# Gated mixers: half-width signed level steps on VectorE without GpSimd, row transposes between the levels, the output norm split by token half

## The chip, the cores and the metric

The kernel runs on one core of one Trainium2 chip, as one launch. The metric is the device time of one execution in microseconds, from its first to its last work on the core; a comparison takes the median of several runs. TensorE multiplies matrices into PSUM (eight banks of 128 x 512 fp32 values), VectorE (DVE), ScalarE (ACT) and GpSimd (POOL) work on rows of 128 partitions, SyncE (SP) starts the DMAs that bring the weights. The engines run programs of their own and meet only at semaphores.

## What is computed

A model of four layers on 256 tokens of width 1024, in fp32: a short convolution with gated DeltaNet, a mixture of 32 experts, a mixer of retention and gated linear attention (GLA), a dense SwiGLU block, an HGRN2 mixer, a mixture of 8 experts, a norm. The change touches the GLA and retention mixer and the HGRN2 mixer, which share this core:

```python
def gated_chunkwise(q, k, v, log_f):          # chunks of 64 tokens
    g_cum = jnp.cumsum(_to_chunks(log_f), axis=-2)
    def step(state, inp):
        qc, kc, vc, gc = inp
        diff = gc[:, :, :, None, :] - gc[:, :, None, :, :]
        decay = jnp.exp(jnp.where(mask, diff, -jnp.inf))
        scores = jnp.einsum('bhid,bhjd,bhijd->bhij', qc, kc, decay)
        g_last = gc[:, :, -1:, :]
        o = (jnp.einsum('bhij,bhjv->bhiv', scores, vc)
             + jnp.einsum('bhid,bhdv->bhiv', qc * jnp.exp(gc), state))
        state = (jnp.exp(g_last[:, :, 0, :])[..., None] * state
                 + jnp.einsum('bhjd,bhjv->bhdv', kc * jnp.exp(g_last - gc), vc))
        return state, o
# hgrn2: o = rms_norm(o, norm_g) * silu(g);  then @ w_out, added to the residual
```

GLA has 4 heads with keys of 64 values and values of 128. HGRN2 has 8 heads of 128, which the kernel takes as two halves of 4 heads. Retention has the same recurrence with a constant decay per head.

## The kernel before

**Layout.** A head's channels lie on the 128 partitions, its 256 tokens along the row; four heads are 1024 columns. Two GLA heads share one 256-column block of keys (`padded`), so that keys, decays and queries are 512 columns; the queries are spread over 1024 with the other head's channels zeroed by a mask.

**Levels.** The pairwise decays inside a chunk of 64 are made in `NL` = 6 levels of block sizes 32, 16, 8, 4, 2, 1, after a round 0 for the diagonal. At level n every block of 2 x size tokens has an older and a newer half. `gated_difference` (L2072) subtracts from the summed log decays g their value at the last token of the older half (the edge), over the full width; `gated_scalar_round` (L2055) makes exp(-|difference|) of it in two activations; `scaled_queries` (L2085, products L2090 and L2095) multiplies the queries by it on VectorE and `gated_pool_round` (L2065, L2069) the keys on GpSimd; `scores` (L2031, L2036) makes 16 matmul instructions of eight 128 x 128 products; `take_scores` (L2113) copies under a mask, with a predicated copy (L2121) over all 1024 columns, the pairs (older key, newer query) of this level into `c_AT`. Round 0 takes the diagonal (L2118). Scores of round n lie in banks 4 and 5 for even n, in 6 and 7 for odd n.

**Behind the levels.** `gated_vector_end` (L2125) makes g minus its last value of the chunk (L2133), the queries times exp(g), and the decays of whole chunks; `gated_scalar_end` (L2143) their exponentials (L2147 to L2151) and, after the transposes, the eviction of the key rows into two masked copies `c_kd` (L2157); `gated_pool_end` (L2161, L2163) the keys for the state; `gated_tensor_end` (L2166) transposes these to rows (`k_rows`, L2173, L2177) and calls `attend_tensor` (L2182).

**Attend.** Four chunks c: the state products Sp (L2198), VectorE's state S (L2239, L2241), the outputs o (L2215 from the state, L2217 from the scores) in banks 6 and 7. Between them `out.fill(1)` puts one quarter of the next projection (L508 to L510) or one block of the output projection (L638). Then the norm over all 1024 columns: square (L2260), sum by a matmul with ones (L2225), Ln and Exp (L2263, L2265), gain and gate on VectorE (L2250, L2253), which is y.

**What runs beside it.** The projections are made of three fp32r matmuls each; for that ScalarE rounds each quarter of a weight piece (`weights_hi_of`, L547) and GpSimd subtracts it from the original (`weights_lo_of`, L557), 128x1024 a piece. In GLA and in the first hgrn half TensorE has half a projection (`proj`) between the scores of two rounds, and in GpSimd's program the products of a round and two weight quarters alternate. On VectorE rounds 4 to 6 of the first hgrn half also have the forget gate of the second (L2846, L2847, reciprocal L2851). In the second half only output blocks lie between the rounds. `cumulate` (L2524) sums the log decays. The order on every engine is the order of its program; SP's loads wait for the last use of their slot.

Of the kernel before, what the change touches and what calls it, by code (L numbers as in the profile page):

```python
# [8 lines left out]
I32 = mybir.dt.int32  # L9
# [130 lines left out]
def program(nc, known, A):  # L140
# [3 lines left out]
    with ctx:  # L144
# [1870 lines left out]
        c_lb, c_omlb = c_small[:, 24:32], c_small[:, 32:40]  # L2015
        NL = len(LEVELS)

        class Gated:
            def __init__(self, st, tag, nb, q, k, g, v, gate, y, gain):
                self.st, self.tag, self.nb = st, tag, nb  # L2020
                self.q, self.k, self.g, self.v, self.gate, self.y, self.gain = q, k, g, v, gate, y, gain
                self.N = nb * T
                self.w = [w[:, 0:self.N] for w in c_w]
                self.kt = c_kt[:, 0:self.N]
                self.padded = nb == 2

        def parity(ap, par):

            return ap.rearrange("p (b r t) -> p b r t", r=2, t=T)[:, :, par, :]

        def scores(pe, x, name, k, q, b0):  # L2031

            for h in range(H4):
                for t in range(NT):
                    kb = k[:, (h if x.nb == 4 else h // 2) * T + t * P:(h if x.nb == 4 else h // 2) * T + t * P + P]
                    mm = nc.tensor.matmul(inst(bank(b0, 2), h, t), kb, inst(q, h, t), start=True, stop=True)  # L2036
            mm.then_inc(*E[x.st].step())
            E[x.st].name(x.tag + name)

        def gated_tensor_round(pe, x, n):  # L2040

            v, tag = V[x.st], x.tag
            b0 = 4 + 2 * (n % 2)
            if n == 0:
                pe.wait_ge(*v.at(tag + "ready"))
                scores(pe, x, "r0", x.k, c_qt if x.padded else x.q, b0)
            else:
                pe.wait_ge(*v.at(f"{tag}q{n}"))
                pe.wait_ge(*G[x.st].at(f"{tag}k{n}"))
                if n >= 2:  # L2050

                    pe.wait_ge(*v.at(f"{tag}taken{n - 2}"))
                scores(pe, x, f"r{n}", x.kt, c_qt, b0)

        def gated_scalar_round(act, x, n):  # L2055
# [4 lines left out]
            nc.scalar.activation(w, w, ACT.Abs).then_inc(*s.step())  # L2060
            act.wait_ge(*s.last())
            nc.scalar.activation(w, w, ACT.Exp, scale=-1.0).then_inc(*s.step())
            s.name(f"{x.tag}w{n}")

        def gated_pool_round(pool, x, n):  # L2065
            pool.wait_ge(*S[x.st].at(f"{x.tag}w{n}"))
            if n >= 2:
                pool.wait_ge(*E[x.st].at(f"{x.tag}r{n - 1}"))
            nc.gpsimd.tensor_tensor(x.kt, x.k, x.w[n % 2], ALU.mult).then_inc(*G[x.st].step())  # L2069
            G[x.st].name(f"{x.tag}k{n}")  # L2070

        def gated_difference(dve, x, n):  # L2072
# [3 lines left out]
            g = x.g.rearrange("p (b i) -> p b i", i=2 * size)  # L2076
            if n >= 3:

                dve.wait_ge(*G[x.st].at(f"{x.tag}k{n - 2}"))
            nc.vector.tensor_tensor(x.w[n % 2].rearrange("p (b i) -> p b i", i=2 * size), g,  # L2080
                                    g[:, :, size - 1:size].to_broadcast([P, x.N // (2 * size), 2 * size]),
                                    ALU.subtract).then_inc(*v.step())
            v.name(f"{x.tag}d{n}")

        def scaled_queries(dve, x, w, scale=1.0):  # L2085

            v = V[x.st]
            if x.padded:
                for par in range(2):
                    ins = nc.vector.scalar_tensor_tensor(  # L2090
                        parity(c_qt, par), x.q.rearrange("p (b t) -> p b t", t=T),
                        consts[:, C_HALF + par:C_HALF + par + 1], w.rearrange("p (b t) -> p b t", t=T),
                        ALU.mult, ALU.mult).then_inc(*v.step())
            else:
                nc.vector.tensor_tensor(c_qt, x.q, w, ALU.mult).then_inc(*v.step())  # L2095

        def gated_vector_round(dve, x, n):
# [3 lines left out]
            if n < NL:  # L2101
                if n >= 1:
                    dve.wait_ge(*v.last())
                gated_difference(dve, x, n + 1)
            if n >= 1:
                dve.wait_ge(*s.at(f"{tag}w{n}"))
                if n >= 2 or x.padded:
                    dve.wait_ge(*e.at(f"{tag}r{n - 1}"))
                scaled_queries(dve, x, x.w[n % 2])
                v.name(f"{tag}q{n}")  # L2110
                take_scores(dve, x, n - 1)

        def take_scores(dve, x, n):  # L2113
            e, v = E[x.st], V[x.st]
            b0 = 4 + 2 * (n % 2)
# [3 lines left out]
            else:  # L2119
                mask = level_mask(n - 1).bitcast(I32).unsqueeze(1).to_broadcast([P, 8, P])  # L2120
                nc.vector.copy_predicated(blocks(c_AT), mask, blocks(bank(b0, 2))).then_inc(*v.step())  # L2121
            v.name(f"{x.tag}taken{n}")
            dve.wait_ge(*v.last())

        def gated_vector_end(dve, x):  # L2125

            e, s, v = E[x.st], S[x.st], V[x.st]
            tag = x.tag
            take_scores(dve, x, NL)

            dve.wait_ge(*G[x.st].at(f"{tag}k{NL}"))
            chunks = x.g.rearrange("p (b i) -> p b i", i=CH)
            nc.vector.tensor_tensor(x.w[0].rearrange("p (b i) -> p b i", i=CH), chunks,  # L2133
                                    chunks[:, :, CH - 1:CH].to_broadcast([P, x.N // CH, CH]),
                                    ALU.subtract).then_inc(*v.step())
            v.name(tag + "last")
# [891 lines left out]
```

## Time and profile before

| | |
|---|---|
| median of 3 runs | 2338.02 us (2336.57 to 2338.24) |
| the profiled execution | 2338.94 us, span of its trace 2337.1 us |
| busy in the span | PE 2045.9 us (88%), DVE 629.3, ACT 502.7, POOL 289.4 |
| chain that ended last | PE 69%, DMA 17%, DVE 8%, ACT 3%, issue 2%, POOL 1% |
| DMA | 653.03 MB, 279 GB/s over the span |

The page gives busy times over the whole span. PE is busy nearly everywhere, but its share differs by stage: the experts are fed at some 420 GB/s, the mixers load little and wait for each other's engines. A row of the chain tells which engine the end of the kernel hung on at that moment; a row of the timeline tells what an instruction waited for.

### The profile page before, as it was taken

Reading aid. Unit: us, or ns where it says so; the run is one execution under the profiler, and the core shown is the slowest. Engines: PE = TensorE matmul, PEld = TensorE weight load, DVE = VectorE, ACT = ScalarE, POOL = GpSimd, SP = SyncE. Lnnn points to the kernel's source line nnn. Section 1 sums busy time; section 2 is a strip of 40 time slices with the busy share of each in tenths; the row PEclk is TensorE's granted clock in tenths of the full one; section 3 lists DMA queues with packets and bytes.
Section 4 is the critical chain, followed back from the end, with each engine's and each line's share of the span. In section 5 each row is a group of like instructions: output and inputs, shape, how many; then the busy total and the mean of one; then the engine's idle time right before and its main releaser. Section 6 shows DMA issues by size and latency. Waiting matters only on the chain.

```text
span 2337.1 us, 38525 instructions
## 1 busy us (share of the span) xinstructions
PE 2045.9 (88%) x16903; PEld 1291.4 (55%) x16903; DVE 629.3 (27%) x983; ACT 502.7 (22%) x641; POOL 289.4 (12%) x118
## 2 busy tenths in 40 slices
PE   6889788787877897999897767999999899999998
PEld 6888544333434886899897655343344334333434
DVE  4662311111112661444377522000001000100101
ACT  3521121211113442343355321000000000000001
POOL 4630000000001560000177310000000000000000
PEclk8999688888888998999998777999999999999999
DMA  7322299999999330355542204899999999999991
GB/s 263 109 109 77 96 424 424 424 424 424 424 424 379 107 110 19 129 179 188 190 145 109 108 1 149 313 388 418 419 417 420 418 419 419 418 420 418 411 390 55
DMA packets 134330, 653.03 MB, mean 279 GB/s; under 512 B 9776, under 2 KB 32432, under 8 KB 88880
## 3 DMA queue, kind: packets, MB, share of 16 engines
q1 hardware_dynamic: 134192, 650.95, 70.0%
q8 instruction: 116, 1.90, 0.3%
q14 instruction: 22, 0.18, 0.0%
HBM read 649.86 MB, written 1.05 MB: 279 GB/s over the span
## 4 chain that ended last, share of the span: by engine, by line
PE 69%; DMA 17%; DVE 8%; ACT 3%; issue 2%; POOL 1%; SPq 0%; POOLq 0%; DVEq 0%; ACTq 0%
PE psum L1748 16%; DMA ring<-in_w_down 14%; PE psum L1810 8%; PE psum L1754 5%; PE psum L508 5%; PE psum L509 5%; PE psum L510 5%; PE psum L638 4%; PE psum L1554 3%; PE psum L1815 3%; DMA ring<-in_moe_w_down 2%; PE psum L2036 2%; PE psum L1775 2%; PE psum L1731 1%; DVE hT L491 1%
## 5 line engine op out<-in xcount | busy, mean ns | idle before, releaser
L1748 PE MATMUL psum<-ring,arena 128*32 128x384 f32 (+1 forms) x3584 | 369.1, 542 | 3.3 <-DMA ring<-in_moe_w_up 2.6
L557 POOL TENSOR_TENSOR ring_r<-ring,ring_r 128x1024 fp32r<-128x1024 f32 x88 | 224.7, 2570 | 969.0 <-ACT ring_r L547 968.9
L510 PE MATMUL psum<-ring_r 128*128 128x256 f32 x1056 | 301.1, 285 | 0.0
L1748 PEld LDWEIGHTS psum<-ring,arena 128*32 128x32 f32 x3584 | 114.3, 110 | 222.5 <-issue 213.0
L508 PE MATMUL psum<-ring_r 128*128 128x256 f32 x704 | 206.8, 294 | 17.5 <-POOL ring_r L557 9.6
L1810 PE MATMUL psum<-ring,arena 128*32 128x512 f32 x1600 | 201.0, 605 | 8.6 <-DMA ring<-in_moe_w_down 8.4
L510 PEld LDWEIGHTS psum<-ring_r 128*128 128x128 f32 x1056 | 205.0, 194 | 0.0
L509 PE MATMUL psum<-ring_r 128*128 128x256 f32 x704 | 201.8, 287 | 0.0
L1954 DVE TENSOR_TENSOR arena<-arena,psum 128x512 f32<-128x512 f32 (+1 forms) x42 | 23.7, 616 | 508.4 <-PE psum L1754 359.4
L1511 PE MATMUL psum<-ring,arena 128*32 128x512 f32 x1024 | 141.9, 707 | 19.6 <-DMA ring<-in_w_up 19.6
L508 PEld LDWEIGHTS psum<-ring_r 128*128 128x128 f32 x704 | 138.4, 197 | 21.0 <-issue 11.4
L1533 PE MATMUL psum<-arena 64*128 64x256 f32 x272 | 99.1, 537 | 45.5 <-ACT arena L1593 45.5
L509 PEld LDWEIGHTS psum<-ring_r 128*128 128x128 f32 x704 | 138.3, 196 | 1.0 <-issue 1.0
L1754 PE MATMUL psum<-ring,arena 128*32 128x512 f32 (+1 forms) x1120 | 131.5, 542 | 0.0
L1893 ACT ACTIVATE arena<-psum 128x512 f32<-128x512 f32 (+1 forms) x42 | 20.0, 544 | 467.0 <-PE psum L1785 467.0
L547 ACT ACTIVATE ring_r<-ring 128x1024 fp32r<-128x1024 f32 x88 | 91.0, 1055 | 119.6 <-PE psum L510 119.6
L1533 PEld LDWEIGHTS psum<-arena 64*128 64x128 f32 x272 | 69.6, 264 | 66.9 <-issue 47.5
L508 PE MATMUL psum<-ring_r,arena_r 128*128 128x256 f32 x352 | 99.9, 284 | 5.5 <-DVE ring_r L533 5.5
L1511 PEld LDWEIGHTS psum<-ring,arena 128*32 128x32 f32 x1024 | 36.3, 127 | 121.0 <-issue 121.0
L638 PE MATMUL psum<-arena,ring 128*128 128x256 f32 x384 | 93.7, 402 | 9.9 <-DVE arena L2253 9.9
L1659 DVE TENSOR_TENSOR xT<-xT,psum 128x512 f32<-128x512 f32 x68 | 46.7, 687 | 206.4 <-PE psum L1533 206.4
L509 PE MATMUL psum<-ring_r,arena_r 128*128 128x256 f32 x352 | 99.8, 283 | 0.0
(370 smaller groups left out, 2779.8 us busy)
## 6 DMA issues: line engine op xcount, KB each, us to landing
ring<-in_w_gate SPq DMA_DIRECT2D x64, 1024.0 KB, 15.8
ring<-in_w_down SPq DMA_DIRECT2D x32, 2048.0 KB, 21.0
ring<-in_w_up SPq DMA_DIRECT2D x64, 1024.0 KB, 19.9
ring<-in_moe_w_gate SPq DMA_DIRECT2D x64, 1024.0 KB, 22.4
ring<-in_moe_w_down SPq DMA_DIRECT2D x64, 1024.0 KB, 21.0
ring<-in_moe_w_up SPq DMA_DIRECT2D x48, 1024.0 KB, 18.8
ring<-in_moe_w_gate SPq DMA_DIRECT2D x64, 768.0 KB, 20.6
ring<-in_moe_w_up SPq DMA_DIRECT2D x48, 768.0 KB, 21.3
```

Of the source, the lines that this page charges most:

```text
L508: nc.tensor.matmul(out, ah, bh, start=start, stop=False, **kw)
L509: nc.tensor.matmul(out, ah, bl, start=False, stop=False, **kw)
L510: return nc.tensor.matmul(out, al, bh, start=False, stop=stop, **kw)
L547: nc.scalar.activation(w_hi[:, :, c], w[:, :, c], ACT.Copy).then_inc(*S[st].step())
L557: nc.gpsimd.tensor_tensor(lo[:, :, c], w[:, :, c], w_hi[:, :, c].bitcast(F32), ALU.subtract)\
L638: mm = nc.tensor.matmul(bank(b // 2)[:, (b % 2) * T:(b % 2 + 1) * T], w[:, k, (b % 4) * P:(b % 4 + 1) * P], self.src[:, k, :], start=(firs ...
L1511: mm = nc.tensor.matmul(bank(0)[s * C:(s + 1) * C, :], q_Xg[:, k * PC + x * C:k * PC + (x + 1) * C], w[s][:, k, :], start=(k == 0), stop=( ...
L1533: mm = nc.tensor.matmul(bank(5 - r % 2)[:, j * T:(j + 1) * T], q_y[:, k * P:(k + 1) * P], q_shareT, start=True, stop=True)
L1554: mm = nc.tensor.matmul(bank(2)[at:at + C, :], q_hidT[:, f * PC + x * C:f * PC + (x + 1) * C], w[x][:, f, half * 512:(half + 1) * 512], st ...
L1748: mm = nc.tensor.matmul(bank(b0 + j)[n * MORE:(n + 1) * MORE, 0:Q], z_Xg[:, x:x + MORE], w[:, (2 * h + j) * Q:(2 * h + j + 1) * Q], start= ...
L1754: mm = nc.tensor.matmul(bank(b0 + 2)[q * MORE:(q + 1) * MORE, 0:Q], z_Xg[:, x:x + MORE], w[:, q * Q:(q + 1) * Q], start=(k == 0), stop=(k ...
L1810: mm = nc.tensor.matmul(bank(6)[tile * MORE:(tile + 1) * MORE, :], z_hidT[:, x:x + MORE], rows_of(half, 0, 512), start=first, stop=last)
```

## The change

- The differences are taken with a sign that is never positive, older half edge - g and newer half g - edge, as two instructions of half width; ScalarE needs one Exp per round and no Abs.
- Queries are scaled in the newer halves and keys in the older halves only, both on VectorE; keys (and for the unpadded mixers queries too) are double-buffered. GpSimd keeps only the weight rounding.
- The predicated copies act on the newer columns alone.
- The difference to the chunk's last value is taken in round 0; its Exp and that of g come in ScalarE's round 1, the state keys in VectorE's round 1, the decayed queries in round 2; the key rows are transposed before the scores of round 3, in banks of their own turn, and evicted after ScalarE's round 3.
- The padded layout puts a head's two masked copies in contiguous halves of 512. Two buffers move into `hT`, which is free in these stages.
- Outputs of chunks 0, 1 and of 2, 3 go to banks 6 and 7; square, sum, Ln, Exp, gain and gate act per token half, and the first half's sum stands between chunks 2 and 3; chunk 2 is given two fills.
- In hgrn the factor of q goes into the keys' factor. The rotation of the retention mixer moves to banks 4 and 5.

```diff
+        BANK_USES = ["r0", "r1", "r2", "kr"] + [f"r{n}" for n in range(3, NL + 1)]
...
+        def wait_for_bank(pe, x, use):
+            at = BANK_USES.index(use)
+            if at >= 2:
+                before_ = BANK_USES[at - 2]
+                pe.wait_ge(*(S[x.st].at(x.tag + "kd") if before_ == "kr" else V[x.st].at(f"{x.tag}taken{before_[1:]}")))
...
         def gated_tensor_round(pe, x, n):
+            if n == 3:
+                pe.wait_ge(*v.at(tag + "kl"))
+                wait_for_bank(pe, x, "kr")
+                k_rows(pe, x, x.kl, bank_of("kr"))
...
         def gated_scalar_round(act, x, n):
-            nc.scalar.activation(w, w, ACT.Abs).then_inc(*s.step())
-            act.wait_ge(*s.last())
-            nc.scalar.activation(w, w, ACT.Exp, scale=-1.0).then_inc(*s.step())
+            nc.scalar.activation(w, w, ACT.Exp).then_inc(*s.step())
             s.name(f"{x.tag}w{n}")
+            if n == 1:
+                act.wait_ge(*v.at(x.tag + "last"))
+                nc.scalar.activation(x.kl, x.kl, ACT.Exp).then_inc(*s.step())
+                s.name(x.tag + "el")
+                nc.scalar.activation(x.eg, x.g, ACT.Exp).then_inc(*s.step())
+                s.name(x.tag + "eg")
...
         def gated_difference(dve, x, n):
+            nc.vector.tensor_tensor(older(w, size), edge, older(x.g, size), ALU.subtract).then_inc(*v.step())
+            nc.vector.tensor_tensor(newer(w, size), newer(x.g, size), edge, ALU.subtract).then_inc(*v.step())
...
         def gated_vector_round(dve, x, n):
+                    dve.wait_ge(*v.at(f"{tag}z{n - 1}" if n >= 2 else f"{tag}last"))
+                gated_difference(dve, x, n + 1)
+            if n == 0:
+                chunks = x.g.rearrange("p (b i) -> p b i", i=CH)
+                nc.vector.tensor_tensor(x.kl.rearrange("p (b i) -> p b i", i=CH),
+                                        chunks[:, :, CH - 1:CH].to_broadcast([P, x.N // CH, CH]), chunks,
+                                        ALU.subtract).then_inc(*v.step())
+                v.name(tag + "last")
+                return
+            dve.wait_ge(*s.at(f"{tag}w{n}"))
+            if x.padded or n >= 2:
+                dve.wait_ge(*e.at(f"{tag}r{n - 1 if x.padded else n - 2}"))
+            if x.padded:
+                masked_queries(dve, x, w, q, lambda ap: newer(ap, size))
+            else:
+                nc.vector.tensor_tensor(newer(q, size), newer(x.q, size), newer(w, size), ALU.mult).then_inc(*v.step())
+            nc.vector.tensor_tensor(older(k, size), older(x.k, size), older(w, size), ALU.mult).then_inc(*v.step())
+            v.name(f"{tag}z{n}")
+            take_scores(dve, x, n - 1)
+            if n == 1:
+                dve.wait_ge(*s.at(tag + "el"))
+                nc.vector.tensor_tensor(x.kl, x.k, x.kl, ALU.mult).then_inc(*v.step())
+                v.name(tag + "kl")
+            elif n == 2:
+                dve.wait_ge(*s.at(tag + "eg"))
+                nc.vector.tensor_copy(c_decay[:, 0:4 * x.nb], x.eg[:, CH - 1::CH]).then_inc(*v.step())
...
+                    nc.vector.tensor_tensor(x.qd, x.q, x.eg, ALU.mult).then_inc(*v.step())
+                v.name(tag + "qd")
...
+                at, new = (newer(ap, size).rearrange("p (n b) i -> p n b i", n=8) for ap in (c_AT, bank(b0, 2)))
+                nc.vector.copy_predicated(at, mask, new).then_inc(*v.step())
...
-        def gated_pool_round(pool, x, n):
-        def gated_vector_end(dve, x):
-        def gated_scalar_end(act, x):
-        def gated_pool_end(pool, x):
-        def gated_tensor_end(pe, x, out=None):
...
         def attend_tensor(pe, x, out=None):
+            def sums(t):
+                pe.wait_ge(*s.at(f"{tag}osq{t}"))
+                mm = nc.tensor.matmul(bank_heads(5 - t), ones[:, :], by_time(c_AT, t), start=True, stop=True)
...
-                    out.fill(1)
+                    out.fill(2 if c == 2 else 1)
...
+                if c == 2:
+                    sums(0)
             if out:
                 out.fill(2)
+            sums(1)
...
         def attend_scalar(act, x):
+            for t in range(NT):
+                at = by_time(c_AT, t)
+                act.wait_ge(*e.at(f"{tag}o{2 * t + 1}"))
+                nc.scalar.activation(at, bank_heads(6 + t), ACT.Square).then_inc(*s.step())
...
-                do(nc.vector.tensor_scalar(x.q, x.q, float(P) ** -0.5, None, ALU.mult))
```

## Rows read from the trace of the kernel before

**Rows 1.** windows: us, busy PE, PEld, DVE, ACT, POOL; PE clock, DMA share, GB/s

```profile
795.00:933.00 138.00, 119.36 (x862) 111.16 (x863) 70.25 (x72) 51.42 (x67) 57.73 (x26) 0.96 0.26 85
1201.00:1395.00 194.00, 144.66 (x953) 132.88 (x953) 105.28 (x102) 74.40 (x79) 93.81 (x32) 0.83 0.22 83
1442.00:2300.00 858.00, 841.58 (x8664) 335.36 (x8665) 60.84 (x124) 60.23 (x124) 0.00 (x0) 0.99 0.97 392
```

**Rows 2.** PE timeline behind the GLA rounds: start, us, what, idle before, releaser

```profile
852.66 1.95 PE L2311 MATMUL psum<-arena,consts 128*128 128x512 f32 x4 [1.57 <-DVE arena L2492]
...
862.15 2.05 PE L2198 MATMUL psum<-arena 128*128 128x128 f32 x16 [1.35 <-ACT arena L2157]
...
865.58 0.35 PE L508 MATMUL psum<-ring_r 128*128 128x256 f32 x1 [1.38 <-ACT ring_r L547]
...
885.51 1.98 PE L2225 MATMUL psum<-arena,ones 128*128 128x512 f32 x4 [1.11 <-ACT arena L2260]
...
892.52 3.75 PE L2036 MATMUL psum<-arena 128*128 128x128 f32 x16 [5.03 <-DVE arena L2253]
...
932.14 15.77 PE L638 MATMUL psum<-arena,ring 128*128 128x256 f32 x64 [4.95 <-DVE arena L2253]
```

**Rows 3.** chain that ended last, first and sixth GLA scores: start, us

```profile
795.50 2.05 PE psum L2036 x16
...
834.02 2.05 PE psum L2036 x16
```

**Rows 4.** the same chain, hgrn first half

```profile
1200.29 0.70 DVE arena L2875
...
1204.07 0.21 PE psum L508
...
1283.46 3.78 PE psum L2198 x16
...
1305.99 1.03 ACT arena L2260
...
1315.16 1.24 DVE arena L2080
```

**Rows 5.** timeline of PE in hgrn, both halves

```profile
1235.70 2.02 PE L2036 MATMUL psum<-arena 128*128 128x128 f32 x16 [0.26 <-issue]
...
1247.96 3.78 PE L2036 MATMUL psum<-arena 128*128 128x128 f32 x16 [3.96 <-DVE arena L2095]
...
1279.83 1.97 PE L2177 MATMUL psum<-consts,arena 128*128 128x128 f32 x8 [8.04 <-POOL arena L2163]
...
1322.18 3.75 PE L2036 MATMUL psum<-arena 128*128 128x128 f32 x16 [5.86 <-POOL arena L2069]
...
1355.45 2.02 PE L2036 MATMUL psum<-arena 128*128 128x128 f32 x16 [1.74 <-issue]
```

**Rows 6.** the same chain, hgrn second half

```profile
1369.35 3.57 PE psum L2198 x16
1372.92 1.73 PE psum L638 x8
...
1385.23 1.03 ACT arena L2260
...
1394.87 16.55 PE psum L638 x64
```

**Rows 7.** DVE groups by form, 1312 to 1358, then 1204 to 1260

```profile
L2121 DVE COPY_PREDICATED arena<-consts,psum 128x1024 f32<-128x1024 int32 x6 | 7.8, 1304 | 3.2 <-PE psum L2036 3.2
L2080 DVE TENSOR_TENSOR arena<-arena 128x1024 f32<-128x1024 f32 x6 | 7.4, 1226 | 4.7 <-POOL arena L2069 4.6
...
L2080 DVE TENSOR_TENSOR arena<-arena 128x1024 f32<-128x1024 f32 x4 | 11.3, 2830 | 3.7 <-POOL arena L2069 3.6
```

**Rows 8.** timeline, 512 columns on ACT and on DVE

```profile
791.91 0.60 ACT L2275 ACTIVATE arena<-psum 128x512 f32<-128x512 f32 x1 [0.81 <-PE psum L510]
...
787.48 0.69 DVE L2473 SCALAR_TENSOR_TENSOR arena<-arena 128x512 f32<-128x512 f32 x1 [1.36 <-ACT arena L2384]
```

More of the change, by code:

```diff
@@ L2143, in gated_scalar_end @@
-        def gated_scalar_end(act, x):
-            s, v = S[x.st], V[x.st]
-            tag = x.tag
-            act.wait_ge(*v.at(tag + "last"))
-            nc.scalar.activation(x.w[1], x.g, ACT.Exp).then_inc(*s.step())
-            s.name(tag + "eg")
-            nc.scalar.activation(x.w[0], x.w[0], ACT.Abs).then_inc(*s.step())
-            act.wait_ge(*s.last())
-            nc.scalar.activation(x.w[0], x.w[0], ACT.Exp, scale=-1.0).then_inc(*s.step())
-            s.name(tag + "el")
-            for b in range(x.N // 512):
-                act.wait_ge(*E[x.st].at(f"{tag}kr{b}"))
-                for half in range(2):
-                    nc.scalar.activation(c_kd[half][:, b * 512:(b + 1) * 512], bank(4 + b), ACT.Copy,
-                                         scale=consts[:, C_HALF + half:C_HALF + half + 1]).then_inc(*s.step())
-            s.name(tag + "kd")
@@ L2220, in attend_tensor @@
                 e.name(f"{tag}o{c}")
+                if c == 2:
+                    sums(0)
             if out:
                 out.fill(2)
-            pe.wait_ge(*s.at(tag + "osq"))
-            for half in range(2):
-                mm = nc.tensor.matmul(bank(4 + half), ones[:, :], c_w[0][:, half * 512:(half + 1) * 512],
-                                      start=True, stop=True)
-            mm.then_inc(*e.step())
-            e.name(tag + "osum")
+            sums(1)
         def attend_vector(dve, x, decay, meanwhile=None):
@@ L2233, in attend_vector @@
                 dve.wait_ge(*e.at(f"{tag}Sp{c}"))
+                if c:
+                    dve.wait_ge(*v.last())
                 if c > 1:
@@ L2392, in mixer2_scalar @@
                     keep(name, halves(out), parts=(part,), **kw)
+                    if n == 3:
+                        gated_scalar_rows(act, GLA)
                     n += 1
@@ L2397, in mixer2_scalar @@
             act.preload_act_table_set(EXP_LN)
-            gated_scalar_end(act, GLA)
             keep("av", halves(a_v))
@@ L2417, in mixer2_pool @@
         def mixer2_pool(pool):
-            def lo(name, quarters=range(4)):
-                weights_lo_of(pool, "mix2", "two", name, quarters)
-            lo("bqk")
-            lo("bv")
-            lo("aq", (0, 1))
-            n = 1
-            for name, after in (("aq", "ak"), ("ak", "bg"), ("bg", "av")):
-                gated_pool_round(pool, GLA, n)
-                lo(name, (2, 3))
-                gated_pool_round(pool, GLA, n + 1)
-                lo(after, (0, 1))
-                n += 2
-            lo("av", (2, 3))
-            gated_pool_end(pool, GLA)
-            lo("ag")
+            for name in ("bqk", "bv", "aq", "ak", "bg", "av", "ag"):
+                weights_lo_of(pool, "mix2", "two", name)
         def mixer2_vector(dve):
@@ L2783, in hgrn_scalar @@
                 gated_scalar_round(act, HG[1], n)
+                if n == 3:
+                    gated_scalar_rows(act, HG[1])
                 if n == 2:
@@ L2787, in hgrn_scalar @@
                     act.preload_act_table_set(EXP_LN)
[L2788 removed]
             attend_scalar(act, HG[1])
         def hgrn_pool(pool):
[L2792 to L2810 removed]
+            for name in ("hf0", "hq0", "hi0", "hg0", "hf1", "hq1", "hi1", "hg1"):
+                weights_lo_of(pool, "hgrn", "two", name)
         def hgrn_vector(dve):
```

224 lines of the change are left out of this document (104 added, 120 removed).

## The prediction

> **What bounds the kernel now.** I read the busy time of three stretches first [rows 1]. In the GLA and retention stretch (795 to 933) TensorE is busy 119 of 138 us; in the two hgrn halves (1201 to 1395) only 145 of 194, at a mean clock of 0.83; in the second mixture of experts (1442 to 2300) 842 of 858 with the DMA engines at 0.97. So the order of waits in the mixers matters, TensorE is what a shorter mixer must free, and the last stage is full from end to end. Then I read TensorE's waits in the GLA stage [rows 2] and its pace there [rows 3]: from the first scores to the sixth, 38.5 us for five rounds, 7.7 us each, of which 2.05 are scores and 5.65 half a projection. That is TensorE at work all the time: the rounds of the GLA stage have nothing to give. Its waits come behind them. For hgrn I read the chain that ended last [rows 4 and 6] and the waits [rows 5]: the reader is to see a wait of 8.0 us for GpSimd's last product, one of 4.0 in round 5, and in the second half the rounds, which have only output blocks beside them.
>
> **GLA and retention.** The rounds stay at 7.7 us. Three waits behind them lose their cause [rows 2]: 1.57 us (the rotated queries are late, because VectorE first waits for ScalarE's exponentials, behind the silu of the gate; these now sit in rounds 1 and 2), 1.35 us (the key rows are evicted) and 1.38 us (ScalarE stood in that eviction and rounded the next weights late). Together 4.3. The transposes are moved and not removed, and what ScalarE now does in round 3 (two copies of 0.6 us) lies beside 5.65 us of projection.
> The norm by halves: square, Ln, Exp and the two VectorE products each act on 512 columns, at 0.60 us on ScalarE and 0.69 on VectorE [rows 8] instead of about 1.05 and 1.25. The half for the first tokens goes under the fourth chunk; its sum is work that is moved. TensorE's wait for the square falls from 1.11 to 0.7, that for y from 5.03 to 2.9 (0.65 + 0.63 + 0.69 + 0.69 and handoffs) [rows 2], which is 2.5. In retention the wait of 4.95 falls to 2.9 likewise, 2.05; one output block is moved ahead of it at no cost. **Sum: 8.9 us.**
>
> **Hgrn, first half.** The scaling of q goes: 0.70 [rows 4], on the chain, since r0 waits for it. From the end of r0 (1204.07 [rows 4]) to r4 (1235.70 [rows 5]) 31.6 us pass. TensorE's own work is four halves of 5.65, three scores of 2.05, the moved transposes (1.0; eight took 1.97 at the half clock [rows 5]) and about 0.9 for matmuls at the lower clock behind r0 (its first took 0.21 us [rows 4]), 30.6: a gain of 1.0. Round 4 is new trouble: ScalarE must make four copies of 0.6 before the exponential of round 4, so VectorE's products come some 8.5 to 10.8 us after the transposes begin and TensorE wants them after 8.8; I take 1.0 off. The wait of 3.96 in round 5 [rows 5] I leave: it comes from the three instructions of the next forget gate (5.9 us), and behind them now stand four half-width instructions where two stood.
> After the last projection TensorE stands from 1271.8 to 1283.46 [rows 5, 4]: for the products of the state keys, then the transposes, then the eviction. All of it is done by round 4 now: 11.6. The first state products then run warm, 2.05 us [rows 2] where they took 3.78 [rows 4]: 1.7. From the last output to the end of y were 9.2 us (1305.99 to 1315.16 [rows 4]); now 1.0 for the moved sum, 0.7, a sum of 1.6 half cold, 2.66 and handoffs, 6.2: 3.0. **Sum: 0.7 + 1.0 − 1.0 + 11.6 + 1.7 + 3.0 = 17.0.** What covers the state keys' rows now is the projections of rounds 3 and 4; if that cover were gone the 2.4 us of copies would come back. Queued behind them on ScalarE are the exponential of round 4 and the rounding of weights.
>
> **Hgrn, second half.** No projection covers it. From the end of y (1315.16) to the first state products (1369.35) are 54.2 us [rows 4, 6]. VectorE now does per round: two half-width differences, two half-width products, each 0.70 (a 128x512 product of two took 0.69 [rows 8], so halves cost more than half of 1.23), and a half-width predicated copy, 1.30 − 0.53 = 0.77 [rows 7]: 3.6 us, no less than the 3.76 of before, but GpSimd's 3.4 us and its two handoffs are gone from the chain. Laid out from the end of y: difference 1, the state difference, difference 2 and products 1 end at 5.4 (r1 began 7.0 after y before [rows 5]); the diagonal copy 1.22, state keys 1.23, difference 3, products 2 at 10.65; copy, decayed queries, difference 4, products 3 and copy at 16.4, when r3 may start. ScalarE's four copies hold its exponential of round 4 until 18.6, products 4 end at 20.0. From there TensorE sets the pace, scores 2.02 [rows 5] and an output block 1.73 [rows 6]: r5 at 23.9, r6 at 27.7, its block done at 31.5. I add 1.5 because the clock is at its lower level after the waits at the start: r1 took 3.75 behind a wait of 5.9 [rows 5]. So 33.0 against 54.2: 21.2. Key rows, the last predicated copy, the exponentials behind it: none stand between r6 and the state products, which were 11.9 us apart (1357.5 to 1369.35). The first state products: 3.57 → 2.05, 1.5. The tail from 1385.23 to 1394.87 [rows 6] was 9.6, now 6.2: 3.4. The output projection after it took 16.55 for 64, where warm blocks of 1.73 would give 13.8; I take nothing, as a wait of 2.9 may keep it cold. **Sum: 26.1.**
>
> **The sum.** 8.9 + 17.0 + 26.1 = 52.0. The profiled execution took 2338.9 us (span 2337.1 and 1.8 around it), the median of the runs is 2338.0; taken off the median it gives 2286. No layer of loading eats it: the loads of the last stage's first weights begin when the hgrn projections free their slots, and move ahead with them; the stage is at its rate from the start [rows 1].
>
> **A rule against the trace.** A 128x1024 product of two SBUF operands took VectorE 1.23 us with GpSimd idle and 2.83 in the mean while GpSimd rounded weights [rows 7]. The Trainium skill ("SBUF — State Buffer", "SBUF: two separate sides") says why: VectorE instructions with two SBUF inputs and GpSimd share a port pair, and the one that starts first holds it for its whole instruction. The trace agrees. It speaks against splitting: each half can be held up anew. It is the first rival.
>
> **Rivals.**
> *The port holds the halves up.* Per round of the GLA stage and of the first hgrn half GpSimd still makes two products of about 2.4 us. If both hold VectorE up in full, its round is 3.6 + 4.8 = 8.4 us against TensorE's 7.7: 0.7 in each of twelve rounds, 8 us: 2294. For it: the 2.83 [rows 7]. Against: a third GpSimd product per round is gone, and one round of slack lies between products and scores.
> *The clock stays low in the second half.* If TensorE's waits of one to two us keep rounds 2 to 6 and the state products cold, scores cost 3.75 and blocks 3.5: five rounds of 7.3 instead of 3.8 to 5, some 13 us: 2299. For it: before, one round fell back (mean clock 0.83 [rows 1]); against, from r4 on TensorE has no wait.
> *It all goes well.* The round 5 wait shrinks by 4, its scores stay warm, the output projection runs warm (2.7 twice), round 4 is not late: 52 + 13, 2273.
> *Short strided runs are slow (the other side).* At the last levels the half-width patterns are runs of one or two values with gaps, which no row of before shows on VectorE. If each half-width instruction took dt longer, the second half loses 30 dt, the first 30 dt, GLA 36 dt less about 12 us of slack; the gain of 52 is eaten at dt = 0.67 us, that is if halves of 0.70 took 1.37, more than the full width did. At 0.8 the kernel would be at 2351. Against it: the full-width differences re-read one value per run at every level, down to runs of two, and all took 1.23 [rows 7]. A cost of 0.1 to 0.2 each is only part of the range. The Trainium skill ("SBUF — State Buffer", "Door 1: The DMA port swizzle") says that a 16-byte SBUF line wants two hits and that a PSUM line has two fp32 values; every second value of a bank is one hit per line, so by it the copy of the last level would be slow, three instructions in all, under 2 us if each took its former 1.30. No run here shows it.
>
> **How the numbers follow.** My forecast 0.50, the port 0.17, the low clock 0.10, all well 0.17, slow strided runs 0.03, gains lost elsewhere (a late weight, a new wait that leaves the time within 0.2% of before) 0.03. The range reaches over the port and low clock cases above and to 2268 below, where the halves would also cost 0.62 rather than 0.70: 2268 to 2302. Within 0.2% (4.7 us, what a measurement of this kernel can tell from no change) only the last case; slower only the strided one, in most of its sizes. Faster 0.95, same 0.02, slower 0.03.
>
> **What would show it.** Right: GpSimd left with weight rounding alone; GLA rounds still 7.7 us apart and no wait over 1 us until its squares; the first state products of the first hgrn half within 1 us of the last projection, those of the second some 33 us after y; waits of 2.9 for y. Wrong: strided products well over 0.70 with GpSimd idle; rounds of the first hgrn half over 8.4 us; a new wait of r3 for the copy before it or of r4 for the evicted rows.

## The result, and the profile after

| | before | after | ratio [95%] |
|---|---|---|---|
| medians (4 runs each) | 2338.13 us | 2285.16 us (2283.60 to 2288.95) | 0.9775 [0.9760, 0.9789] |
| predicted | | 2286 us (2268 to 2302) | |
| profiled execution | 2338.94, span 2337.1 | 2288.95, span 2287.0 | |

The kernel is faster by 53 us, one microsecond from the forecast. The sum behind it was less right than that: two of its terms missed, one by 5 us, and others made up for it. The spans, cut at instructions that both kernels have (PE's first GLA scores, its retention scores, the output projection of the retention mixer, VectorE's first scan, the end of y of the first hgrn half, the last output projection and its end), each number the difference of two starts:

| us | before | after | gain | forecast | paced (below) |
|---|---|---|---|---|---|
| up to the GLA scores | 795.5 | 795.5 | 0.0 | 0 | 795.3 |
| GLA | 97.0 | 95.5 | 1.5 | 6.8 | 88.8 |
| retention | 39.6 | 36.4 | 3.2 | 2.1 | 37.2 |
| output projection, dense block, forget gate | 260.8 | 259.3 | 1.5 | 0 | 259.0 |
| hgrn, scans to the first y | 122.2 | 107.0 | 15.2 | 17.0 | 95.4 |
| hgrn, second half | 79.7 | 51.2 | 28.5 | 26.1 | 50.5 |
| its output projection | 16.6 | 15.8 | 0.8 | 0 | 15.6 |
| all behind it | 925.7 | 926.3 | −0.6 | 0 | 924.5 |

The windows of after that answer to [rows 1] (columns as there) show TensorE with the same instructions in shorter stretches, at a mean clock of 0.92 in hgrn where it was 0.83, and VectorE and GpSimd with less work. (Warm and cold below stand for TensorE's two clock levels: the sixteen matmuls of a round's scores took 1.8 to 2.05 us warm and up to 3.8 cold.)

```profile
795.00:928.00 133.00, 119.19 (x863) 112.34 (x864) 56.91 (x89) 48.05 (x66) 44.50 (x19) 0.95 0.26 88
1195.00:1345.00 150.00, 129.47 (x953) 123.80 (x953) 92.89 (x138) 60.57 (x71) 41.70 (x17) 0.92 0.28 106
```

**GLA.** PE's waits in its timeline after, where [rows 2] had 1.57, 1.35, 1.38, 1.11, 5.03 and 4.95:

```profile
807.21 3.78 PE L2066 MATMUL psum<-arena 128*128 128x128 f32 x16 [3.96 <-DVE arena L2165]
...
886.81 1.12 PE L2239 MATMUL psum<-arena,ones 128*128 128x512 f32 x2 [0.69 <-ACT arena L2305]
...
890.98 3.51 PE L2066 MATMUL psum<-arena 128*128 128x128 f32 x16 [3.04 <-DVE arena L2297]
...
927.42 15.77 PE L638 MATMUL psum<-arena,ring 128*128 128x256 f32 x64 [2.95 <-DVE arena L2297]
```

The first three waits are gone and the norm's shrank as forecast. New is the first row: round 1 waits 3.96 us for VectorE's keys, and its scores then take 3.78 us where those of [rows 3] took 2.05. That is 5.7 us, more than the 5.3 by which the stage misses its forecast. VectorE's and GpSimd's timelines say why; the last line is GpSimd's in the kernel before:

```profile
795.98 2.87 DVE L2150 TENSOR_TENSOR hT<-arena 128x512 f32<-128x512 f32 x1
798.89 2.52 DVE L2129 TENSOR_TENSOR arena<-arena 128x256 f32<-128x256 f32 x1
801.33 0.41 DVE L2130 TENSOR_TENSOR arena<-arena 128x256 f32<-128x256 f32 x1
...
804.60 2.56 DVE L2165 TENSOR_TENSOR arena<-arena 128x256 f32<-128x256 f32 x1
```
```profile
795.92 5.20 POOL L557 TENSOR_TENSOR ring_r<-ring,ring_r 128x1024 fp32r<-128x1024 f32 x2 [0.82 <-ACT ring_r L547]
801.61 2.39 POOL L557 TENSOR_TENSOR ring_r<-ring,ring_r 128x1024 fp32r<-128x1024 f32 x1 [0.49 <-ACT ring_r L547]
```
```profile
798.60 1.29 POOL L2069 TENSOR_TENSOR arena<-arena 128x512 f32<-128x512 f32 x1 [3.43 <-ACT arena L2062]
```

A subtraction of 256 columns takes 0.41 us in one row and 2.52 in another: beside a weight quarter of GpSimd it waits that quarter out. Before the change GpSimd's program had its level product between the quarters, and so waited for ScalarE's exponentials there, 3.43 us before the one of round 1. Now it has only weights and runs through four quarters while VectorE is in rounds 0 and 1.

**First hgrn half.** VectorE's scans and GpSimd beside them (timelines), first before, then after:

```profile
1192.93 7.33 DVE L2524 TENSOR_TENSOR_SCAN arena<-ones,arena 128x64 f32<-128x64 f32 x16 [1.13 <-ACT arena L2754]
```
```profile
1193.92 4.73 POOL L557 TENSOR_TENSOR ring_r<-ring,ring_r 128x1024 fp32r<-128x1024 f32 x2 [5.01 <-ACT ring_r L547]
```
```profile
1186.74 11.56 DVE L2555 TENSOR_TENSOR_SCAN arena<-ones,arena 128x64 f32<-128x64 f32 x16 [1.13 <-ACT arena L2787]
```
```profile
1187.73 9.32 POOL L557 TENSOR_TENSOR ring_r<-ring,ring_r 128x1024 fp32r<-128x1024 f32 x4 [5.01 <-ACT ring_r L547]
```

PE's waits (timeline) and the chain that ended last, both after:

```profile
1198.35 3.71 PE L2066 MATMUL psum<-arena 128*128 128x128 f32 x16 [7.69 <-DVE arena L2555]
...
1244.16 3.78 PE L2066 MATMUL psum<-arena 128*128 128x128 f32 x16 [5.32 <-DVE arena L2165]
```
```profile
1267.80 1.78 PE psum L2232 x16
...
1293.74 0.60 DVE arena L2129
```

The first state products start as the last projection ends, at 1267.80 and warm (1.78 us); before they came 11.7 us after it and took 3.78 [rows 4]. Against that the sixteen scans take 11.56 us, with four weight quarters beside them, where they took 7.33 with two. TensorE's wait before round 0 is 7.69 us now.

**Second hgrn half**, same chain:

```profile
1309.66 2.42 ACT arena L2118 x4
1312.09 0.95 ACT arena L2103
...
1313.67 0.70 DVE arena L2165
1314.41 2.05 PE psum L2066 x16
...
1325.22 1.78 PE psum L2232 x16
```

From y (1293.74) to the first state products are 31.5 us where [rows 4, 6] had 54.2. Round 4 is set by ScalarE: its exponential comes behind the four copies of the key rows. From there TensorE does its rounds without a wait, 3.5 us each.

### The profile page after: what moved, and what is told of

It reads as the page before. It is cut to its first block and busy times, and to the rows that moved or that the text cites. A ratio compares the mean times of both kernels' runs of the same rounds, so it can differ in the third digit from the quotient of the medians.

```text
span 2287.0 us, 38522 instructions
## 1 busy us (share of the span) xinstructions
PE 2032.6 (89%) x16903; PEld 1283.9 (56%) x16903; DVE 604.3 (26%) x1029; ACT 486.2 (21%) x632; POOL 226.7 (10%) x97
## 5 line engine op out<-in xcount | busy, mean ns | idle before, releaser
L557 POOL TENSOR_TENSOR ring_r<-ring,ring_r 128x1024 fp32r<-128x1024 f32 x88 | 214.8, 2452 | 1020.2 <-ACT ring_r L547 1020.1
L1748 PEld LDWEIGHTS psum<-ring,arena 128*32 128x32 f32 x3584 | 114.5, 110 | 223.0 <-issue 212.8
L1511 PEld LDWEIGHTS psum<-ring,arena 128*32 128x32 f32 x1024 | 36.6, 128 | 122.2 <-issue 122.2
L1810 PEld LDWEIGHTS psum<-ring,arena 128*32 128x32 f32 x1600 | 52.5, 111 | 77.7 <-issue 58.2
```

What stands on the lines that cost most here:

```text
L557: nc.gpsimd.tensor_tensor(lo[:, :, c], w[:, :, c], w_hi[:, :, c].bitcast(F32), ALU.subtract)\
L1511: mm = nc.tensor.matmul(bank(0)[s * C:(s + 1) * C, :], q_Xg[:, k * PC + x * C:k * PC + (x + 1) * C], w[s][:, k, :], start=(k == 0), stop=( ...
L1748: mm = nc.tensor.matmul(bank(b0 + j)[n * MORE:(n + 1) * MORE, 0:Q], z_Xg[:, x:x + MORE], w[:, (2 * h + j) * Q:(2 * h + j + 1) * Q], start= ...
L1810: mm = nc.tensor.matmul(bank(6)[tile * MORE:(tile + 1) * MORE, :], z_hidT[:, x:x + MORE], rows_of(half, 0, 512), start=first, stop=last)
```

## The experiments

All were timed against the kernel before on the same chip. Three chips were used. The runs with GpSimd held back once, with the whole norm and with the late key rows shared one with after's second run; the second paced run and the two at the end shared another with its third. The first paced run and those on the key products, the forget gate and the full-width copies had no run of after beside them, so there the ratios are compared.

**After, a second and a third time**, as the base of the comparisons on their chips.

> The changed kernel once more, on the chip of the three variants sent with it. It ought to give 2285 us within 3 us; it sets what the others are compared with.

> The changed kernel a third time, beside the paced ones on their chip: 0.977 of the kernel before, within 0.002.

2282.72 us (2280.84 to 2285.39), 0.9765 [0.9745, 0.9786], and 2283.66 (2280.52 to 2285.06), 0.9763 [0.9750, 0.9776].

**GpSimd held back once in each mixer.**

```diff
+            weights_lo_of(pool, "mix2", "two", "aq", (0, 1))
+            pool.wait_ge(*V["mix2"].at("bz1"))
+            weights_lo_of(pool, "mix2", "two", "aq", (2, 3))
...
+            weights_lo_of(pool, "hgrn", "two", "hg0", (0, 1))
+            pool.wait_ge(*V["hgrn"].at("h0z1"))
+            weights_lo_of(pool, "hgrn", "two", "hg0", (2, 3))
```

> GpSimd makes the third quarter of the first weight piece after round 0 only when VectorE's products of round 1 are done, in the GLA stage and in the first hgrn half. Theory A (GpSimd's weight rounding, no longer spaced by its level products, holds VectorE up through the shared port): the wait of 3.96 us and the cold scores behind it in the GLA round 1 go (5.7 us), the sixteen scans of hgrn fall from 11.6 us to about 7.3 (4.2 us): about 10 us less than the changed kernel, 2275. Rival B (VectorE is late in round 1 by its own longer program, the state difference and the halves): under 2 us, 2283 to 2285.

2286.23 us (2284.44 to 2288.04), 0.9780 [0.9760, 0.9800]: no faster than after (2282.72). The waits left where they were expected to leave (the scans are back at 7.33 us, r1 of GLA waits no more) and came back one round later. GpSimd, then VectorE, then PE:

```profile
798.59 15.30 POOL L557 TENSOR_TENSOR ring_r<-ring,ring_r 128x1024 fp32r<-128x1024 f32 x6 [4.01 <-DVE arena L2165]
```
```profile
801.48 2.60 DVE L2129 TENSOR_TENSOR arena<-arena 128x256 f32<-128x256 f32 x1
...
806.54 5.15 DVE L2136 SCALAR_TENSOR_TENSOR arena<-arena,consts 128x256 f32<-128x256 f32 x2
811.61 2.56 DVE L2165 TENSOR_TENSOR arena<-arena 128x256 f32<-128x256 f32 x1
```
```profile
814.23 3.78 PE L2066 MATMUL psum<-arena 128*128 128x128 f32 x16 [3.96 <-DVE arena L2165]
```

GpSimd had six quarters waiting and made them without a gap, and five VectorE instructions that take 2.1 us alone took 12.9 (one of 2.62 is left out here). The mechanism is shown; that one wait would be enough was wrong.

**GpSimd held back at every pair of quarters**, a wait for the products of round n before the pair that takes their place in its program.

```diff
+            for name, after in (("aq", "ak"), ("ak", "bg"), ("bg", "av")):
+                pool.wait_ge(*V["mix2"].at(f"bz{n}"))
+                weights_lo_of(pool, "mix2", "two", name, (2, 3))
+                pool.wait_ge(*V["mix2"].at(f"bz{n + 1}"))
+                weights_lo_of(pool, "mix2", "two", after, (0, 1))
+                n += 2
```

(and the same in hgrn, for `h0z{n}`)

> GpSimd waits for VectorE's products of round n before the n-th pair of weight quarters, as its own level products paced it before, in the GLA stage and the first hgrn half. Theory A (a stretch of GpSimd instructions back to back holds up every VectorE instruction with two SBUF inputs for one of them; pairs with a pause hold up two per round): the GLA wait of 3.96 us and its cold scores go, the scans take 7.3 us instead of 11.6 and the wait of 4.38 in round 2 that the single delay made does not come: 8 to 10 us less than the changed kernel (2283 on the chip of the first four), about 2274. Rival B (any delay of GpSimd comes back, as with the single delay): 2281 to 2287.

> GpSimd's weight quarters in pairs behind VectorE's products, as in the paced run, now on one chip with the changed kernel. By theory A and the places found in its trace (GLA 5.7 us, up to r0 of hgrn 5.6, its rounds 5.4), 13 to 17 us less than the changed kernel; if the 15 us of the first comparison came from the chip, under 10.

2267.95 us (2263.29 to 2273.09), 0.9711 [0.9693, 0.9729]; and 2265.99 (2263.98 to 2268.02), 0.9690 [0.9677, 0.9703], 17.7 us under after on the same chip (by the intervals of the ratios, good to some 4 us). That is theory A, which expected 8 to 10 us in the first run and 13 to 17 in the second. In the second run's timeline no GLA round waits for VectorE, r0 of hgrn waits 3.45 us and r5 0.70, where after had 7.69 and 5.32:

```profile
1180.15 7.32 DVE L2565 TENSOR_TENSOR_SCAN arena<-ones,arena 128x64 f32<-128x64 f32 x16 [1.13 <-ACT arena L2797]
```
```profile
1187.53 2.05 PE L2066 MATMUL psum<-arena 128*128 128x128 f32 x16 [3.45 <-DVE arena L2565]
...
1227.07 2.05 PE L2066 MATMUL psum<-arena 128*128 128x128 f32 x16 [0.70 <-DVE arena L2165]
```

The table above has its stages in the last column: the gain over after lies in GLA (6.8) and in the first hgrn half (11.6), the two places that have GpSimd beside VectorE. The edit touches nothing but GpSimd's waits, so this is what its free run costs the changed kernel.

**The norm over all 1024 columns again**, transposes and levels as after.

```diff
-                    out.fill(2 if c == 2 else 1)
+                    out.fill(1)
...
-            for t in range(NT):
-                y = by_time(x.y, t)
-                dve.wait_ge(*s.at(f"{tag}orstd{t}"))
-                nc.vector.scalar_tensor_tensor(y, bank_heads(6 + t), x.gain, by_time(c_AT, t), ALU.mult, ALU.mult)\
...
+            dve.wait_ge(*s.at(tag + "orstd"))
+            nc.vector.scalar_tensor_tensor(x.y, bank(6, 2), x.gain, c_w[1], ALU.mult, ALU.mult).then_inc(*v.step())
```

> The output norm is whole again, with one fill per chunk, everything else as changed. Theory A (each tail after the last output loses its length from the halves): GLA +2.5, retention +2, first hgrn half +3.6, second +4.0, about 12 us more than the changed kernel, 2297. Rival B (the first half's sum on TensorE gives back most of it): at most 5 us more, 2290.

2299.02 us (2295.03 to 2300.82), 0.9833 [0.9811, 0.9854]: 16 us more than after. The waits of before return (PE timeline):

```profile
893.28 3.75 PE L2066 MATMUL psum<-arena 128*128 128x128 f32 x16 [4.96 <-DVE arena L2294]
...
1354.21 16.36 PE L638 MATMUL psum<-arena,ring 128*128 128x256 f32 x64 [4.87 <-DVE arena L2294]
```

The profiled execution is 16.7 us longer than that of after's second run, and the stages place it: 9.8 us in the mixers and their output projections, 2.1 in the stretch of the dense block, 2.5 ahead of the first GLA scores and 2.4 behind the last output projection. In the last three the edit changes nothing, so about 10 us are the norm's by the trace.

**The key rows behind the levels again**, their products where after has them.

```diff
-            if n == 3:
-                pe.wait_ge(*v.at(tag + "kl"))
-                wait_for_bank(pe, x, "kr")
-                k_rows(pe, x, x.kl, bank_of("kr"))
...
+            if x.g is not None:
+                pe.wait_ge(*v.at(tag + "kl"))
+                wait_for_bank(pe, x, "kr")
+                k_rows(pe, x, x.kl, bank_of("kr"))
```

(with ScalarE's eviction behind round 6, and the rotation in banks 6 and 7)

> The state keys are still made in round 1, but their transposes and the eviction come behind round 6 again, with the banks of before. Theory A (moving the transposes is worth its waits): GLA +2.7, first hgrn half +4.5, second +2.5, about 10 us more than the changed kernel, 2295. Rival B (what counted was to have the state keys early; the transposes and four copies cost about the same wherever they stand, since early they hold up round 4): at most 4 us more, 2289.

2298.80 us (2296.53 to 2300.42), 0.9832 [0.9811, 0.9853]: again 16 us more, of which the profile shows about 12 in the mixers; as with the norm, the rest lies ahead of them and behind them. PE timeline:

```profile
865.04 2.05 PE L2231 MATMUL psum<-arena 128*128 128x128 f32 x16 [1.35 <-ACT arena L2113]
...
1274.51 3.62 PE L2231 MATMUL psum<-arena 128*128 128x128 f32 x16 [4.07 <-ACT arena L2113]
...
1334.32 2.05 PE L2231 MATMUL psum<-arena 128*128 128x128 f32 x16 [2.07 <-ACT arena L2113]
```

The first is the row of [rows 2], and the 1.38 us behind it is back too; in the first hgrn half the state products wait 4.07 us and run cold.

**The kernel before, with only its key products moved to VectorE**, at full width.

```diff
+                nc.vector.tensor_tensor(x.kt, x.k, x.w[n % 2], ALU.mult).then_inc(*v.step())
+                v.name(f"{tag}k{n}")
...
-                gated_pool_round(pool, GLA, n)
```

> The kernel before with one part of the change: GpSimd's key products go to VectorE at full width, nothing else. Theory A (off GpSimd alone gives little: VectorE then has 5.0 us of work per hgrn round and 4.1 per GLA round, each with two GpSimd quarters in its way; second hgrn half 8 to 10 us less, GLA and first half 5 to 12 more): 2330 to 2345. Rival B (GpSimd's removal is the main source of the gain): 2315 or less.

2336.54 us (2332.63 to 2341.54), 0.9998 [0.9987, 1.0009]: no change. In the second half it does what was wanted: from y to the first state products 45.3 us instead of 54.2. What it gains there it loses where GpSimd now runs free: again four quarters stand in a row behind the first GLA scores, and the sixteen scans take 11.55 us. PE timeline:

```profile
807.70 3.41 PE L2036 MATMUL psum<-arena 128*128 128x128 f32 x16 [4.21 <-DVE arena L2113]
...
1209.97 3.66 PE L2036 MATMUL psum<-arena 128*128 128x128 f32 x16 [8.41 <-DVE arena L2851]
...
1255.91 3.75 PE L2036 MATMUL psum<-arena 128*128 128x128 f32 x16 [6.37 <-DVE arena L2113]
```

So taking GpSimd out of the chain gains nothing by itself in this kernel, as theory A had it. What it is worth with GpSimd held back no run shows, and none has the differences and products of after at full width, so the share of the half widths in the gain stays open.

**The next forget gate all in round 5**, so that it doesn't stand ahead of round 5's products.

```diff
-                if n == 4:
+                if n == 5:
                     forget_start(1)
-                    forget_reciprocal(1, 0, 1)
-                elif n == 5:
-                    forget_reciprocal(1, 1, 2)
...
-                    forget_reciprocal(1, 3, 1)
+                    forget_reciprocal(1, 0, H4)
```

> The forget gate of the second hgrn half starts after VectorE's round 5 and its reciprocal is one instruction after round 6. Theory A (the wait of 5.32 us and the cold scores of round 5 come from these instructions in round 4): 6 to 7 us less than the changed kernel, about 2276. Rival B (the 6.6 us reciprocal behind round 6 is late for the state of the first half, so the gain is given back): at most 2 us less, 2281.

2279.56 us (2277.54 to 2283.35), 0.9757 [0.9742, 0.9773], an interval that holds the ratios of after's second and third run (0.9765 and 0.9763): at most a few us, and not the 6 to 7 of theory A. By the profile the wait of 5.32 us is gone, but the half up to its last sum is only 2.6 to 2.9 us shorter than in the three executions of after. The gate's end now meets GpSimd (VectorE's timeline; these two took 3.1 us together in after), and PE waits for it:

```profile
1255.37 5.29 DVE L2878 SCALAR_TENSOR_TENSOR arena<-arena 128x256 f32<-128x256 f32 x4
1260.69 5.39 DVE L2884 TENSOR_SCALAR arena<-arena 128x256 f32<-128x256 f32 x4
```
```profile
1266.94 2.08 PE L2232 MATMUL psum<-arena 128*128 128x128 f32 x8 [2.27 <-DVE arena L2282]
```

**The predicated copies over the full width again.**

```diff
-                mask = newer(level_mask(n - 1), size).bitcast(I32).unsqueeze(1)\
-                    .to_broadcast([P, 8, P // (2 * size), size])
-                at, new = (newer(ap, size).rearrange("p (n b) i -> p n b i", n=8) for ap in (c_AT, bank(b0, 2)))
+                mask = level_mask(n - 1).bitcast(I32).unsqueeze(1).to_broadcast([P, 8, P])
```

> The changed kernel with the predicated copies over all 1024 columns again (0.6 us more for each of eighteen). Theory A (only VectorE's chain up to round 4 of the second hgrn half pays, and the rounds held up by GpSimd a little): 2 to 4 us more than the changed kernel, 2285 to 2287. Rival B (each copy is on the path): 10 us more, 2293.

2285.10 us (2280.84 to 2287.00), 0.9777 [0.9761, 0.9792], which nothing tells from after: theory A's 2 to 4 us more is too little to be told, rival B's 10 is not there. VectorE's groups in the second half, 1294 to 1330, first of after, then of this kernel:

```profile
L2196 DVE COPY_PREDICATED arena<-consts,psum 128x512 f32<-128x512 int32 x6 | 5.4, 904 | 3.1 <-PE psum L2066 3.1
L2164 DVE TENSOR_TENSOR arena<-arena 128x512 f32<-128x512 f32 x6 | 4.1, 686 | 3.6 <-ACT arena L2103 3.6
```
```profile
L2193 DVE COPY_PREDICATED arena<-consts,psum 128x1024 f32<-128x1024 int32 x6 | 7.8, 1296 | 2.1 <-PE psum L2066 2.1
```

The copies do take 2.4 us less as halves; they stand behind the products in VectorE's program, and its waits beside them shrink by as much (3.1 and 3.6 us to 2.1 and 2.5): that time was slack.

**Paced, with ScalarE's exponential of round 4 ahead of the eviction of the key rows** in the second half; and that, with GpSimd's first gate quarters held until VectorE's scans are done.

```diff
-                if n == 3:
+                if n == 4:
                     gated_scalar_rows(act, HG[1])
...
+            pool.wait_ge(*V["hgrn"].at("h0ready"))
```

(the first edit alone, then both)

> Paced, and in the second hgrn half ScalarE makes the exponential of round 4 ahead of the eviction of the key rows. Theory A (the 0.83 us wait of the scores of round 4 comes from that eviction in front of the exponential): the first state products come 1 to 1.5 us earlier after the end of y than the 31.5 us of the changed kernel. Rival B (round 4 needs the evicted rows as well, so the order is the same to it): no difference.

> As the one before, and GpSimd also holds the first pair of the gate weights of hgrn until q and k are ready. Theory A (the scans on the way to round 0 then take 3.0 us instead of 7.3, TensorE's wait of 3.45 before round 0 goes, 1 to 2 us come back as waits for the first weight quarter and for round 1): 1.5 to 3 us less than paced and swapped. Rival B (all of it comes back in round 1): no difference or 1 us more.

2268.05 us (2267.71 to 2271.05), 0.9702 [0.9689, 0.9715], and 2267.41 (2265.09 to 2269.57), 0.9696 [0.9683, 0.9709]: both no faster than paced (2265.99). In place both do what they should. With the swap the 0.83 us wait before r4 is gone and y to the state products shrinks from 30.8 to 30.3 us, too little to count. With the scans alone on VectorE, they take 3.03 us instead of 7.32, but the quarters then fall on the next instructions (VectorE's timeline, the second kernel):

```profile
1180.37 3.03 DVE L2565 TENSOR_TENSOR_SCAN arena<-ones,arena 128x64 f32<-128x64 f32 x16 [1.13 <-ACT arena L2797]
...
1184.04 2.85 DVE L2130 TENSOR_TENSOR arena<-arena 128x512 f32<-128x512 f32 x1
1186.82 3.42 DVE L2150 TENSOR_TENSOR hT<-arena 128x1024 f32<-128x1024 f32 x1
```

Round 1's scores come 2.5 us earlier than in paced, those of round 5 after a wait of 1.30 us for VectorE instead of 0.70, 0.4 us earlier: the gain at the start is given back by round 5.

## Why the prediction was right, and where it was not

**The second half, 26.1 forecast, 29.3 measured with its output projection.** The layout held at its ends: r3's scores 16.3 us after y (16.4), state products at 31.5 (33.0), every half-width difference and product at 0.69 us. Between them it was two errors that cancelled: VectorE was done at 14.5 us, two early, and TensorE, with r1 and r2 cold, used that up. Round 4 waits only 0.8 us, for the reason given. The surplus lies in the state products and the tail, 5.8 us where 4.9 were forecast, in the 1.5 us added for the low clock, which were not needed, and 0.8 in the output projection, at which I had taken nothing.

**The first half, 17.0 forecast, 15.2 measured.** The step "11.6" held (11.7 to 0.1), "1.7" measured 2.0, the tail "3.0" 3.6, the rounds gave 1.4 net where I had nothing net, though the wait of round 5 grew by as much. The step that failed is the first, "the scaling of q goes: 0.70": it went, but the scans ahead of it, which I had not counted as touched, took 4.2 us more. The trace of before had the row of it, 7.33 us for sixteen scans of 64 columns beside two quarters; I read it as their price. They take 3.03 alone. The mean of 2.83 us in [rows 7] (of L2080, which makes the differences, not products) hid the same thing: three of the four took 3.3 us.

**GLA, 6.8 forecast, 1.5 measured.** The three waits and the norm came as stated. The step that failed is "the rounds stay at 7.7 us": r2 to r6 do, but r1's scores end 5.7 us late. I had priced the port as "0.7 in each of twelve rounds" if two GpSimd products hold VectorE up, "against: one round of slack". Slack there is from round 2 on; round 1 has none, and just there GpSimd, freed of the level product that made it wait, runs four quarters in a row. The price assumed that GpSimd keeps to two instructions per round, and that failed. Not the number of GpSimd's instructions decides, but where they stand: with the same quarters in the same order, but held to the rounds, the kernel is 17.7 us faster.

**The port rival** (2294) named the right mechanism and priced it at less than half: 8 us, where the paced kernel puts it at 17.7. Not all of that is new. The 3.96 us wait of round 5, which the forecast left in and put down to the forget gate alone, is in good part this same cost and was there before (of 5.32 us after, pacing leaves 0.70). What is new the forecast had at nothing, and it came out near the median because retention, the second half and stretches that no edit touches gave more than it counted. That one microsecond is luck; the waits behind the rounds and the second half, which are most of the sum, are not. The rivals of the low clock, of short strided runs and of gains lost did not come: of the scores of the second half only those of rounds 1 and 2 ran at the lower clock (3.75 and 3.78 us), and the strided differences and products cost 0.69 us at every level. The rule on PSUM lines of the Trainium skill ("SBUF — State Buffer", "Door 1: The DMA port swizzle") would make the last level's predicated copy slow. It was, but so was the one before, see below, and the run with all copies at full width shows no cost.

**Parts.** Put back alone, the norm by halves is worth 16 us (about 10 in place), the early key rows 16 (about 12 in place), the half-width copies nothing; by the intervals of the ratios either 16 is good to some 5 us. The rest of the 53, with the half-width differences and products, the single exponential and the double buffers, was not put back alone. Open are the four to five us of either that lie outside the mixers, the 1.5 us that the stretch around the dense block got shorter by, which no edit touches, and the 0.6 behind the mixers. That stretch is 1.5 to 2.4 us shorter in each of three profiled executions of after, but there is only one of before. The three differ by 4 us up to their last output projection, so a difference of that size may be no finding.

## What to carry to other kernels

When work is taken off an engine, ask what its waits had held back: GpSimd's level product was also the brake that kept its weight quarters from running in a row beside VectorE's rounds, and the kernel without it ran 17.7 us slower than with the brake put back as bare waits. Where two engines exclude each other per instruction, place the long instructions of one in the idle stretches of the other, at every round and not once. And price a freed chain by its first round, which has no slack ahead of it.

## What the runs showed of the hardware

**The hold between VectorE and GpSimd is per instruction and doesn't shrink with the width.** Beside 128x1024 subtractions of GpSimd (2.4 us alone, 2.55 in the run of six), VectorE's two-operand instructions took up to 2.6 us at 256 columns (0.41 alone), 2.87 at 512 (0.69), 3.42 at 1024 (1.22): 2.2 us more at each width. It reaches further than differences and products of two SBUF operands: the scans, and a copy of eight columns in the paced kernel, the row below (0.15 us alone), and TENSOR_SCALAR of 256 columns above (5.39 for four against 1.38).

```profile
806.94 1.98 DVE L2174 COPY arena<-hT 128x8 f32<-128x8 f32 x1
```

The Trainium skill ("SBUF — State Buffer", "SBUF: two separate sides") has the rule, that whichever starts first keeps the shared port pair for its whole instruction, and the traces agree.

**Predicated copies from PSUM with gaps.** Of 512 columns they took 0.69 to 0.74 us at block sizes 32 to 4 and 1.30 to 1.33 at 2 and 1, as much as the 1.30 of all 1024 columns (VectorE's timeline of after, levels 4 and 5):

```profile
1244.02 0.69 DVE L2196 COPY_PREDICATED arena<-consts,psum 128x512 f32<-128x512 int32 x1
...
1249.20 1.32 DVE L2196 COPY_PREDICATED arena<-consts,psum 128x512 f32<-128x512 int32 x1
```

Subtractions and products of SBUF operands with the same gaps stay at 0.69. By the line of two values that the Trainium skill gives for PSUM ("SBUF — State Buffer", "Door 1: The DMA port swizzle") I had expected it at size 1 alone; at size 2 the measurement decides, and I have no cause for it.

**The clock after a wait is not fixed by its length.** After 3.45 us without work the sixteen scores took 2.05 us in the paced kernel (above) and 2.97 in the one with the swap:

```profile
1187.53 2.97 PE L2066 MATMUL psum<-arena 128*128 128x128 f32 x16 [3.45 <-DVE arena L2565]
```

The mean granted clock from 1187.5 to 1189.5 was 1.00 in the first and 0.74 in the second. With the same program up to there, the scores of round 1 came 1.6 us later by it: differences of one or two microseconds between single traces of these kernels say nothing.
